# Gate rows by way of DRAM: TensorE's products with the unit matrix and ScalarE's copies replaced by transfers, in a two-block sequence model on one core

## What is computed

```python
for i in range(DEPTH):
    mod = c_act @ ada_w[i] + ada_b[i]
    sh1, sc1, gt1, sh2, sc2, gt2 = jnp.split(mod, N_MOD, axis=-1)
    h = _modulate(_rmsnorm(x, norm_g[i, 0]), sh1, sc1)
    y = short_conv_mixer(h) if i == 0 else rwkv7_mixer(h)
    x = x + gt1[:, None, :] * y
    h = _modulate(_rmsnorm(x, norm_g[i, 1]), sh2, sc2)
    x = x + gt2[:, None, :] * (jnp.square(jax.nn.relu(h @ mlp_w1[i])) @ mlp_w2[i])
```

## Time and profile before

| what | value |
|---|---|
| median of three runs | 1352.4 us |
| profiled execution, its own time | 1350.53 us |
| span of the profiled execution | 1348.8 us |
| PE busy | 1303.3 us (97%), 10507 instructions |
| PEld busy | 1129.8 us (84%) |
| DVE busy | 948.8 us (70%) |
| ACT busy | 701.5 us (52%) |
| POOL busy | 128.3 us (10%) |
| mean granted TensorE clock | 0.998 |
| transfers | 256.90 MB, mean 190 GB/s |

### The profile page before, as it was taken

How to read it: one execution, slowest core, us unless ns; L and a number is a source line. 1 busy time by engine, 2 the same in 40 slices (tenths; PEclk the granted TensorE clock), 3 DMA queues, 4 the chain that set the end, 5 groups by cost and what they waited for, 6 DMA issues and landing times. The chain is left out here.

```text
span 1348.8 us, 24952 instructions
## 1 busy us (share of the span) xinstructions
PE 1303.3 (97%) x10507; PEld 1129.8 (84%) x10507; DVE 948.8 (70%) x1433; ACT 701.5 (52%) x1211; POOL 128.3 (10%) x133
## 2 busy tenths in 40 slices
PE   4999999999999999999999999999999999999997
PEld 2998888998899897788888887888888998888886
DVE  1887788976768776675566888666656677756655
ACT  2544544434567555564444648654445566644443
POOL 0000000010200764100000042000000021000000
PEclk9999999999999999999999999999999999999999
DMA  9996799995341012356665532465555543565561
GB/s 362 372 363 237 299 356 380 352 343 167 115 156 64 4 35 97 95 176 201 188 189 176 182 113 91 148 206 192 187 190 160 174 139 126 172 188 194 183 197 50
DMA packets 177575, 256.90 MB, mean 190 GB/s; under 512 B 10488, under 2 KB 122552, under 8 KB 177464
## 3 DMA queue, kind: packets, MB, share of 16 engines
q1 hardware_dynamic: 177464, 255.31, 56.8%
HBM read 254.25 MB, written 1.05 MB: 189 GB/s over the span
## 5 line engine op out<-in xcount | busy, mean ns | idle before, releaser
L1514 DVE TENSOR_TENSOR w_lo<-stage,w_hi 128x1024 fp32r<-128x1024 f32 (+1 forms) x372 | 447.6, 1239 | 160.4 <-ACT w_hi L889 160.0
L889 ACT ACTIVATE w_hi<-stage 128x1024 fp32r<-128x1024 f32 (+1 forms) x378 | 380.1, 1049 | 211.7 <-PE acc L2318 191.9
L2316 PE MATMUL acc<-w_hi,z_hi 128*128 128x512 f32 x640 | 252.6, 395 | 1.6 <-DVE z_lo L1963 1.6
L2318 PE MATMUL acc<-w_hi,z_lo 128*128 128x512 f32 x640 | 249.4, 390 | 0.0
L2317 PE MATMUL acc<-w_lo,z_hi 128*128 128x512 f32 x640 | 249.2, 389 | 0.0
L2259 PE MATMUL un<-h_both,w_hi 128*128 128x256 f32 x736 | 214.3, 291 | 1.8 <-POOL w_lo L860 1.1
L2260 PE MATMUL un<-h_both,w_hi 128*128 128x256 f32 x736 | 208.1, 283 | 0.0
L2261 PE MATMUL un<-h_both,w_lo 128*128 128x256 f32 x736 | 208.0, 283 | 0.0
L2259 PEld LDWEIGHTS un<-h_both,w_hi 128*128 128x128 f32 x736 | 140.8, 191 | 9.5 <-issue 5.4
L2316 PEld LDWEIGHTS acc<-w_hi,z_hi 128*128 128x128 f32 x640 | 120.1, 188 | 27.8 <-issue 4.0
L2260 PEld LDWEIGHTS un<-h_both,w_hi 128*128 128x128 f32 x736 | 141.0, 192 | 1.2 <-issue 0.7
(11 more groups left out here) (393 smaller groups left out, 1886.0 us busy)
## 6 DMA issues: line engine op xcount, KB each, us to landing
stage<-in_mlp_w SPq DMA_DIRECT2D x64, 1024.0 KB
ada_buf<-in_ada_w SPq DMA_DIRECT2D x48, 1024.0 KB, 11.4
stage<-in_w_up SPq DMA_DIRECT2D x32, 1024.0 KB
stage<-in_w_down SPq DMA_DIRECT2D x32, 1024.0 KB
stage<-in_conv_w_in SPq DMA_DIRECT2D x12, 1024.0 KB
stage<-in_rw_w_rkv SPq DMA_DIRECT2D x12, 1024.0 KB
stage<-in_w_in_a SPq DMA_DIRECT2D x8, 1024.0 KB
stage<-in_w_kv_b SPq DMA_DIRECT2D x8, 1024.0 KB
```

The lines of the kernel that those rows point to most:

```text
L889: A_(w_hi[u % 2][:, half, 0:n], stage[u % NSTAGE][:, half, 0:n], ACT.Copy).then_inc(hi_made, 1)
L1514: V.tensor_tensor(w_lo[u % 2][:, half, 0:n], stage[u % NSTAGE][:, half, 0:n], w_hi[u % 2][:, half, 0:n].bitcast(F32), ALU.subtract).then_i ...
L2316: MM(y, z_hi[:, kt, q], wh[:, i, :], start=(first and kt == 0), stop=False, skip_group_check=True)
L2318: ins = MM(y, z_lo[:, kt, q], wh[:, i, :], start=False, stop=(last and kt == KT - 1), skip_group_check=True)
```

## The change

The gate goes from `mods` to a buffer `gate_kept` in DRAM (4 x 1024) and from there, broadcast, to the same tiles `gate_rows`. SP issues `keep_gate(r)` before units 14, 32, 41 and 60, and `spread_gate(r)` before units 15, 33, 66 and (row 3) 68. PE's `row_of_columns`, ACT's `row_copy` and the waits on both go; DVE waits for `gate_spread` instead. At the place of row 3, `unread` goes from 2 to 6; at the places of rows 0, 1 and 2 nothing takes the products' place.

```diff
+        GATE_SETS = (2, 5, 8, 11)
+        KEEP_GATE_AT = (14, 32, 41, U_RWO)
+        SPREAD_GATE_AT = (15, 33, U_RWO + 6)
...
+            def keep_gate(r):
+
+                sp.wait_ge(ada_added, ADA_ORDER.index(GATE_SETS[r]) + 1)
+                c0 = 8 * (GATE_SETS[r] % 6)
+                sp.dma_start(gate_kept[r].rearrange("(t q) -> q t", q=P), mods[GATE_SETS[r] // 6][:, c0:c0 + KT],
+                             allow_slow_non_contiguous=True).then_inc(sem("gate_written"), 16)
+
+            def spread_gate(r):
+
+                sp.wait_ge(sem("gate_written"), 16 * (r + 1))
+                sp.dma_start(gate_rows[r][:], gate_kept[r].unsqueeze(0).to_broadcast([P, D])).then_inc(sem("gate_spread"), 16)
...
                     sp.dma_start(final_row[:], row_of(VEC_FINAL)).then_inc(sem("final_row_in"), 16)
+                    spread_gate(3)
...
+                if u in KEEP_GATE_AT:
+                    keep_gate(KEEP_GATE_AT.index(u))
+                if u in SPREAD_GATE_AT:
+                    if u == U_RWO + 6:
+                        sp.wait_ge(sem("bonus_gated"), len(GN_GROUPS))
+                    spread_gate(SPREAD_GATE_AT.index(u))
                 load_unit(u)
...
-                            if m == 0 and g == GROUPS - 1:
-                                row_copy(1, stat_ps, misc)
...
-                if j == 9:
-                    row_copy(0, acc[0], acc[1])
...
-            row_copy(2, stat_ps, misc)
             last_splits(U_RWO, N_MLP1)
             norm_split(N_MLP1, gain[:, 3, :], mods[1][:, 24:32], U_MLP[1] + 1)
-            row_copy(3, stat_ps, misc)
...
-                    dve.wait_ge(row_out, row + 1)
+                    dve.wait_ge(gate_spread, 16 * (row + 1))
...
-                            if m == 1 and g == 0 and j == 1:
-                                pe.wait_ge(row_out, 4)
                             up_unit(u + 2 * UPD * g + j, up_pair[j % 2], ready)
-                    if m == 0 and g == GROUPS - 1:
-                        pe.wait_ge(ada_added, LAST_SET)
-                        row_of_columns(1, mods[0][:, 40:48], stat_ps, misc)
...
-                if j == 9:
-                    pe.wait_ge(ada_added, 3)
-                    row_of_columns(0, mods[0][:, 16:24], acc[0], acc[1])
-            pe.wait_ge(row_out, 1)
             last_units(U_CONV_OUT, z_ready(Z_CONV))
...
             output_rows(4)
-            row_of_columns(2, mods[1][:, 16:24], stat_ps, misc)
             wide_unit(U_RWO + 2, 1, rwo_ready, rows=range(0, 2))
...
             keep_warm(V_MLP[1], 1)
-            pe.wait_ge(row_out, 3)
-            row_of_columns(3, mods[1][:, 40:48], stat_ps, misc)
-            unread(un[V_MLP[1] % 2], 2)
+            unread(un[V_MLP[1] % 2], 6)
             turn_first(N_MLP1)
...
+    gate_kept = nc.dram_tensor("gate_kept", (4, D), F32, kind="Internal").ap()
```

More of the change, by code:

```diff
@@ L98, in constant_table, with build @@
     return t
-def build(nc, A, out):
+def build(nc, A, out, gate_kept):
     with ExitStack() as ctx:
@@ L707, in build @@
         xs_low_made, xs_high_made, turned, first_done = (sem(n) for n in ("xs_low_made", "xs_high_made", "turned", "first_done"))
-        row_done, row_out, out_made, final_made = (sem(n) for n in ("row_done", "row_out", "out_made", "final_made"))
+        gate_written, gate_spread, out_made, final_made = (sem(n) for n in ("gate_written", "gate_spread", "out_made", "final_made"))
         scaled_made, sq_f_ready, both_ready, square_ready, root_row_done, root_row_out, tables_made = (
@@ L1037, in norm_split @@
                     split(later)
[L1039 to L1043, removed]
             def z_split(zc, j):
@@ L2351, in turn_next @@
                     turn_tile(n, 4 + t, 1)
[L2353 to L2358, removed]
             def unread(bank, n):
@@ L2377, in turn_raw @@
                     pe.wait_ge(x_ready, x_done(n) - 4 + half)
-                if tiles[0] == 0 and n == N_A:
-                    pe.wait_ge(row_out, 4)
                 for t in tiles:
@@ L2521, in _ @@
             mlp(0, N_MLP0)
-            pe.wait_ge(row_out, 2)
             free_bank(V_RKV + 1)
@@ L3030 @@
     arrays["in_vec_table"] = np.concatenate([np.reshape(inputs[n], (-1, P)) for n in VECTORS])
+    gate_kept = nc.dram_tensor("gate_kept", (4, D), F32, kind="Internal").ap()
     aps = {n[3:]: nc.dram_tensor(n, a.shape, mybir.dt.from_np(a.dtype), kind="ExternalInput").ap() for n, a in arrays.items()}
     out = nc.dram_tensor("out_x", (1, SEQ, D), F32, kind="ExternalOutput").ap()
-    build(nc, aps, out)
+    build(nc, aps, out, gate_kept)
     return run_bass_kernel_spmd(nc, [arrays], core_ids=[0]).results[0]["out_x"]
```

## The result

The changed kernel takes 1356.14 us (median of 6 runs, 1355.49 to 1357.80) against 1351.06 (6 runs) for the kernel before on the same chip: a ratio of 1.0039, 95% interval 1.0026 to 1.0052. It is 0.39% slower, outside the predicted range. The profiled execution took 1357.8 us, with a span of 1356.0.

The account below looks back on a forecast made before the run. PE's own queue was taken as the path. Terms -1.8 - 1.7 + 0 + 1.2 - 0.3 = -2.6, plus 1.7 for a clock fall, gave -0.9: 1351.5 us for the median, range 1348.4 to 1353.8.

Parts of the forecast that it names:

- Row 0: 16 product instructions on PE from 96.67 us go and PE continues with ready work: -1.8 us.
- row 1: Products on PE from 308.88 us go, with a wide unit ready behind them: -1.7 us; other end 1.0 gained.
- row 2: Products at 552.38 us go, but PE waits for DVE's z_lo anyway, some 3.3 us instead of 1.42: gain 0.
- row 3: Six unread products replace two fillers, the row products and four fillers at 567.60 us; transposes come later: +1.2 us.
- ACT's copy: The last removed copy ends at 581.35 us, and PE waits for it before the second up unit: -0.3 us.
- the clock at row 2: PE's 3.3 us gap makes the granted clock fall to half: +1.7 us, ends 0 and 2.1.
- my 1.07: Other end of the gain at row 0: DVE's limited slack lets only 1.07 us of 1.81 through.
- The transfers ... Value: 0: Four writes in 1024 4-byte pieces (about 0.7 us each) and four 512 KB read-backs cost nothing where the queue has time.
- SP starves the weights: SP waits before unit 33 for pieces landing 16.9 us after issue, so PE lacks weights: 1355.1 or more, chance 0.10.
- the 6.6 of cover: Unit 33's load lands at about 231.7 us and ACT wants it at 238.30, so SP may be 6.6 us late.
- The last of the prediction's own signs of being wrong: The prediction is wrong if the trace shows ACT's L889 (L911 after the change) waiting for a load.
- The upper end of the range: 1353.8 us: the forecast with the clock's 2.1, 1.07 at row 0, 1.0 at row 1, and 1.4 for spread.

Follow-up runs that it names:

- the way back late: The changed kernel with the second read-back of a gate issued before unit 40 in place of unit 33: 1352.07 us, ratio 1.0008.
- both ways back late: Changed kernel, third write at unit 59, three unread products at row 2, four at row 3, first two read-backs at units 16 and 40: 1348.58 us, ratio 0.9985.
- the last version but one: Changed kernel with the third write at unit 59, three unread products at row 2 and four in place of six at row 3: 1349.39 us, ratio 0.9982.

## Why the prediction was wrong

- **Row 0, row 1, row 2, row 3, ACT's copy, and the clock at row 2** were right in mechanism and nearly in size: -0.92 measured against -0.9, in part because an error of 0.3 in row 0 cancels 0.3 of the others. Row 0 gave -1.81 at once and kept 1.48; from trace to trace it keeps between -0.4 and 1.5. What takes it back is not DVE in PE's second output unit, as my 1.07 had it: 0.33 goes in every trace without PE's row products where PE waits for ACT's `ada_row` (0.23 at 103.28 us in the changed kernel), and in two of them (the way back late, and both ways back late) PE waits 1.5 and 1.7 us more for a modulation piece behind the first write. Where the third write does no harm, the kernel's time bears the rest out roughly: ratios 0.9997 and 0.9984, that is 0.4 and 2.2 us faster.
- **The step that failed is "The transfers ... Value: 0".** The estimate of 10 ns for a piece was good (9 measured), but it priced the sending alone. The row it was taken from, U_F's 64-byte rows, is a read; the operation that was new was a write of 4 bytes side by side, and after it the other transfers of the queue nearly stop for 6 to 8 us (24 to 86 GB/s). Behind the third write that cost PE 6.06 us. I had a lower bound of nothing and an upper bound from a transfer of another kind, and called that both sides.
- **"SP starves the weights"**, the rival on the slower side, came out in sign and size (1355.1 or more) and not in its place, so its size is luck. SP's rows at `keep_gate(1)`:

```profile
208.19 0.37 SPq L666 DMA_DIRECT2D gate_kept<-mod  x1
...
226.54 0.46 SPq L647 DMA_DIRECT2D stage<-in_mlp_w  x1
```

  The write was in DRAM at 226.14, 18.0 us after its issue. That is longer than the 16.9 of the rival, but the 16.9 counted from 213.61, and the write was issued 5.4 us sooner; the time from which PE would go without weights, 226.9, wasn't reached. Unit 33 was issued at 226.54, 6.2 us late and inside the 6.6 of cover, and its last part landed 8.4 us later, not 11.4, at 234.90; ACT took it at 237.17 without a wait for it. PE lost 0.15 near 270 us. The loss came at the third write, which I had passed over because nobody waits for it. A transfer costs not only those who wait for it; here it cost those queued behind it. The last of the prediction's own signs of being wrong is the one that stands in the trace: ACT's L911 waits 7.2 us for a load.
- The upper end of the range is mis-added: +0.9 is what its terms make against the kernel before (-1.07 - 1.0 + 1.2 - 0.3 + 2.1), and it was added to the forecast. By its terms the end is 1352.4 + 0.9 + 1.4 = 1354.7 in place of 1353.8; the 1356.14 lies above both.
- The fixed part of 2 us that I cited from the Trainium skill ("DMA: Bandwidth & Descriptors", "Anatomy of one DMA") is what the page fits to transfers issued by way of GpSimd; SP's here come near it with the pieces apart (2.5 to 2.9 us) and not with those side by side (7.7 after the last piece was sent). Its remark that the receipt of a write can take surprisingly long is the one that held.

## What to carry to other kernels

Price a new transfer by what it does to the queue behind it, not by who waits for it: look at GB/s by window after its issue, where a DMA share near 1 with few GB/s is a stop. Don't write 4-byte pieces side by side into DRAM while a queue is full; put them apart (256 bytes were tried in a full queue, 32 in an idle one only), write 32 bytes at a time, or do it where nothing is queued behind. Products that look idle may hold the clock: where a stand of 3 us took their place, 2.7 us of unread products brought 1.6 us back.

## What was not expected of the hardware

- 1024 writes of 4 bytes side by side: 7.7 us from the last piece sent to the last receipt, with nothing else moving; 2.5 to 2.9 us in all when 32 to 256 bytes lie between them; 1.42 for the same bytes in pieces of 32.
- A row of 128x512 fp32 read by DVE with a stride of 8 numbers: 1.07 to 1.17 us against 0.69.
- The clock also falls where PE stands only about 1 us twice in 3 us (near 340 us, in the changed kernel and in four of the runs here, not in the profile of the kernel before, with the same idle times), and each such fall sets PE back by 1.6 to 1.7 us. Other traces have one near 464 us (three) or near 816 us (four). Most of the spread between runs of one kernel goes with the clock: of the 33 runs of the kernel before beside the last version but one, those with a mean clock of 0.999 have a median of 1350.3, those with 0.996 one of 1353.1.
